# Nine more seven-product units in a two-block transformer forward pass on one NeuronCore

## The chip, the core and the metric

The kernel runs on one core of one Trainium2 chip. The metric is the device time of one execution in microseconds (us). Shorter is better.

## What is computed

Two blocks, on 256 tokens of width 2048, in float32. Cut to the matrix products that matter here:

```python
# first block
h = rms_norm(x, norm_mix_pre)
p, q, k, v, g_lr, r, gate_logits = split_combined(h @ w_in)      # 2048 x 11280
y_a = pool_mixer(p) @ w_branch_a                                 # 1024 x 2048
y_b = (rms_norm(gla(q, k, v, ...)) * silu(r)) @ w_branch_b        # 2048 x 2048
gates = sigmoid(gate_logits + b_branch_gates)                    # two gates of 2048 columns
mixed = (gates[0] * y_a + gates[1] * y_b) @ w_out                # 2048 x 2048
x = x + rms_norm(mixed)
h = rms_norm(x)
x = x + rms_norm((silu(h @ w_ffn_gate) * (h @ w_ffn_up)) @ w_ffn_down)   # 2048 x 5632
# second block, twice
z = rmsnorm(x) @ w_in_2[l]
y = concat(mla_attention, short_gated_conv, memory_attention) * silu(gate)
x = x + rmsnorm(y @ w_o_2[l])                                    # 2048 x 2048
```

## The kernel before

**Steps.** Each big product is a row of groups, each 512 output columns wide: `ga0` to `ga3` and `gb0` to `gb3` are the two gates, `ya`/`yb` the branches, `wo` the product with `w_out`, `fg`/`fu` feed-forward's gate and up, `d` its down product, `o00` to `o13` the output products of the two layers of the second block. `weight_groups` (line 98) writes them down in order. A step is one k-tile (128 rows) of one group. Both operands are split in a high and a low half of float32 (fp32r), so that a step is 3 matmuls (high by high, low by high, high by low; lines 1120 to 1122) for each of the two halves of the tokens: 6 matmuls of 128x512. Before, there are 1600 steps.

**Slabs.** Weights come in by DMA in pieces of 128x1024 (two k-tiles) into six `raw` buffers. For every piece, a slab, ScalarE (ACT) copies the high half into `wh` (line 1671) and VectorE (DVE) subtracts it to make the low half `wl` (line 2523). There are four slots for slabs, so that ACT can begin a slab only when TensorE (PE) has ended the one four places before. ACT and DVE each go through the slabs in order and between two slabs do what else is due: `background` and `results` are generators that yield a step number, and what follows a yield is put in the engine's queue ahead of the first slab that lies more than three slabs (`AHEAD`) beyond that step. So the order within each engine's queue is fixed when the program is built.

**Units.** In feed-forward, 16 times, the first four k-tiles of two neighbouring groups are not multiplied as 16 quarter products (8 steps) but as 7 (Winograd's form of Strassen's method), in 7 steps: `b11`, `b21`, `t1`, `t3`, `b22`, `t2`, `t4` (`FORMS`). A step of a unit is also 6 matmuls (lines 1041 to 1043), but has a slab of its own. So a unit has 7 slabs where 8 steps had 4. For the `t` slabs DVE first forms differences of raw weights in place (line 2517, four to a unit). The activations' sums and differences (`sform`) are made once for each set of four k-tiles by `forms` on DVE (five operations at lines 1798 to 1805, then the low half at line 1809) with `forms_high` on ACT between. In `seven` (line 1008) the first product `b11`, and every later one whose output lies in a bank `pb`, waits for semaphore `s_l`, the low half of these forms. Four products land in the banks `pb4` to `pb7`; `first_taken` (ACT, line 1206) and `gathered` (DVE, line 1811, four additions) add them up, and `joined` (line 1829) adds what the remaining k-tiles gave.

**The places of the change.** After each `yb` group DVE multiplies its result by the gate (line 2398), adds the two branches (line 2402), and, except after `yb3`, turns the sum with 16 small transposes (`turn`, lines 1688 to 1699) and makes its low half. After `yb3` it computes the tables of angles (`rope_tables`, line 1925) and the last low halves of `mixT`, the input of `wo` (line 1727). During `o00` and `o01` DVE and ACT also split the memory's activations (`memory_low`, `memory_high`). The results of `wo0` to `wo2` and `o00` to `o02` are squared by ACT and multiplied from the accumulator by DVE (`scaled_out`, line 1773).

Of the kernel before, what the change touches and what calls it, by code (L numbers as in the profile page):

```python
# [86 lines left out]
class Group:  # L87
# [3 lines left out]
    def __init__(self, name, act, cols, kts, per=2, gain=None, swap=False, ev=("d", 2)):  # L91
# [3 lines left out]
        self.pair = self.joins = self.forms = None  # L95


def weight_groups(a):
# [29 lines left out]
    def gate_up(part):
        c0, n = PARTS[part]
        w_g, w_u = a["w_ffn_gate"][0], a["w_ffn_up"][0]  # L130
        for c in range(c0, c0 + n):
# [4 lines left out]
            add(f"fu{c}", "x2T", w_u, 512 * c, kts=kts)

    def down(part):
        c0, n = PARTS[part]
        rows = a["w_ffn_down"][0][c0 * 512:(c0 + n) * 512, :]  # L140
        for c in range(4):
            if part < 3 and c % 2 == 0:
                seven(f"ds{part}{c}", f"fT{part % 2}", (f"d{part}{c}", f"d{part}{c + 1}"),
                      [rows[:, 512 * i:512 * i + 512] for i in (c, c + 1)], part + 1)
            add(f"d{part}{c}", f"fT{part % 2}", rows, 512 * c, kts=range(4 if part < 3 else 0, 4 * n), ev=("d", 2))
# [2453 lines left out]
```

## Time and profile before

| | |
|---|---|
| median of 3 runs | 2280.22 us (2280.21 to 2281.05) |
| the profiled execution, its own time | 2281.4 us |
| its span, first to last instruction | 2279.4 us |
| PE busy | 2267.1 us, 10645 instructions |
| DVE busy | 1648.4 us, 2158 instructions |
| ACT busy | 1227.9 us, 1599 instructions |
| granted TensorE clock, mean | 0.999 |

The profiled execution took 1.2 us more than the median, and 2.0 us of it lie outside the span. A matmul's recorded duration (389 ns) overlaps the next one's; the pace is the distance from one start to the next. The same holds for DVE, where one operation's record overlaps the next by some 0.08 us.

### The profile page before, as it was taken

How to read it: one execution, taken by the hardware profiler on the slowest of the kernel's cores; microseconds unless marked ns; L12 is line 12 of the kernel's file. 1: busy time of each engine (PE TensorE's matmuls, PEld its weight loads, DVE VectorE, ACT ScalarE, POOL GpSimd, SP SyncE). 2: the span in 40 equal slices, each digit the busy share in tenths (PEclk: the TensorE clock that was granted, in tenths of full speed). 3: DMA queues.
4: the chain of work that ended last, by engine and by line, in shares of the span. 5: the costliest groups of instructions: out<-in, count | busy, mean ns of one | idle time of the engine just before them, and what ended most of it. 6: DMA issues, size and time to landing. Idle time of an engine off the chain costs nothing.

```text
span 2279.4 us, 27834 instructions
## 1 busy us (share of the span) xinstructions
PE 2267.1 (99%) x10645; PEld 1897.2 (83%) x10645; DVE 1648.4 (72%) x2158; ACT 1227.9 (54%) x1599; POOL 30.5 (1%) x40
## 2 busy tenths in 40 slices
PE   9999999999999999999999999999999999999998
PEld 7888888888888888888888888888888888888887
DVE  6677777756666668898888988875668756676864
ACT  6555655444445755555555555565655446556443
POOL 0000000000000000000000000000000000000000
PEclk9999999999999999999999999999999999999999
DMA  8666665766668557756665776766565665656654
GB/s 295 179 194 197 194 192 166 228 202 202 194 202 275 176 163 251 241 192 226 219 200 174 244 228 213 251 206 197 160 180 166 223 209 148 203 163 182 173 198 136
DMA packets 261604, 458.34 MB, mean 201 GB/s; under 512 B 23808, under 2 KB 63744, under 8 KB 260832
## 3 DMA queue, kind: packets, MB, share of 16 engines
q1 hardware_dynamic: 260192, 453.94, 63.8%
q0 software_dynamic: 848, 2.10, 0.6%
q8 instruction: 84, 1.38, 0.2%
q10 hardware_dynamic: 432, 0.53, 0.1%
q14 instruction: 48, 0.39, 0.1%
HBM read 437.09 MB, written 4.19 MB: 194 GB/s over the span
## 4 chain that ended last, share of the span: by engine, by line
PE 92%; DVE 5%; DMA 1%; ACT 1%; issue 1%; SPq 0%; DVEq 0%; ACTq 0%
PE pm L1120 27%; PE pm L1122 27%; PE pm L1121 27%; PE pb L762 1%; DVE wl L2509 1%; DVE wl L2523 1%; PE pb L1041 1%; PE pb L944 1%; PE pb L1042 1%; PE pb L1043 1%; DVE raw L2517 1%; PE pm L1042 1%; PE pm L1041 1%; PE pm L1043 1%; PE pb L842 1%
## 5 line engine op out<-in xcount | busy, mean ns | idle before, releaser
L2523 DVE TENSOR_TENSOR wl<-raw,wh 128x1024 fp32r<-128x1024 f32 (+2 forms) x722 | 866.2, 1208 | 500.0 <-ACT wh L1671 496.8
L1671 ACT ACTIVATE wh<-raw 128x1024 fp32r<-128x1024 f32 (+2 forms) x722 | 749.4, 1044 | 734.8 <-PE pm L1122 665.0
L1120 PE MATMUL pm<-wh,hTh 128*128 128x512 f32 x702 | 275.1, 392 | 0.8 <-DVE wl L2523 0.8
L1121 PE MATMUL pm<-wl,hTh 128*128 128x512 f32 x702 | 273.3, 389 | 0.0
L1122 PE MATMUL pm<-wh,hTl 128*128 128x512 f32 x702 | 273.3, 389 | 0.0
L1120 PE MATMUL pm<-wh,xT3h 128*128 128x512 f32 (+1 forms) x640 | 249.0, 389 | 0.0
L1122 PE MATMUL pm<-wh,xT3l 128*128 128x512 f32 (+1 forms) x640 | 244.6, 382 | 0.0
L1121 PE MATMUL pm<-wl,xT3h 128*128 128x512 f32 (+1 forms) x640 | 244.4, 382 | 0.0
L1120 PE MATMUL pm<-wh,x2Th 128*128 128x512 f32 x544 | 211.6, 389 | 0.0
L1121 PE MATMUL pm<-wl,x2Th 128*128 128x512 f32 x544 | 211.6, 389 | 0.0
L1122 PE MATMUL pm<-wh,x2Tl 128*128 128x512 f32 x544 | 211.6, 389 | 0.0
L1666 ACT ACTIVATE wh<-raw 128x1024 fp32r<-128x1024 f32 x112 | 118.7, 1061 | 116.7 <-PE pm L1122 87.3
L1120 PEld LDWEIGHTS pm<-wh,hTh 128*128 128x128 f32 x702 | 131.8, 188 | 28.8 <-DVE wl L2523 2.2
L1122 PEld LDWEIGHTS pm<-wh,hTl 128*128 128x128 f32 x702 | 131.8, 188 | 27.7
L1121 PEld LDWEIGHTS pm<-wl,hTh 128*128 128x128 f32 x702 | 131.9, 188 | 26.5
L2509 DVE TENSOR_TENSOR wl<-raw,wh 128x1024 fp32r<-128x1024 f32 x112 | 135.4, 1220 | 18.6 <-ACT wh L1666 17.5
L1122 PEld LDWEIGHTS pm<-wh,xT3l 128*128 128x128 f32 x640 | 120.1, 188 | 23.1
L1121 PEld LDWEIGHTS pm<-wl,xT3h 128*128 128x128 f32 x640 | 120.4, 188 | 20.4
L1120 PEld LDWEIGHTS pm<-wh,xT3h 128*128 128x128 f32 x640 | 120.4, 188 | 20.5
L1120 PEld LDWEIGHTS pm<-wh,x2Th 128*128 128x128 f32 x544 | 102.1, 188 | 21.3
L1122 PEld LDWEIGHTS pm<-wh,x2Tl 128*128 128x128 f32 x544 | 102.1, 188 | 21.2
L1121 PEld LDWEIGHTS pm<-wl,x2Th 128*128 128x128 f32 x544 | 102.1, 188 | 21.1
(512 smaller groups left out, 3760.8 us busy)
## 6 DMA issues: line engine op xcount, KB each, us to landing
raw<-in_w_in SPq DMA_DIRECT2D x286, 512.0 KB, 4.0
raw<-in_w_ffn_gate SPq DMA_DIRECT2D x88, 512.0 KB, 4.9
raw<-in_w_ffn_up SPq DMA_DIRECT2D x88, 512.0 KB, 5.7
raw<-in_w_ffn_down SPq DMA_DIRECT2D x88, 512.0 KB, 5.1
raw<-in_w_o SPq DMA_DIRECT2D x64, 512.0 KB, 4.3
raw<-in_w_in SPq DMA_DIRECT2D x68, 256.0 KB, 3.3
raw<-in_w_branch_b SPq DMA_DIRECT2D x32, 512.0 KB, 4.2
raw<-in_w_out SPq DMA_DIRECT2D x32, 512.0 KB, 4.5
```

The source lines that it names most:

```text
L762: ins = e.transpose(pb[b][:, o:o + 128], src[half], ident[:, :])
L842: ins = e.matmul(pb[4 + i][:, j * 128:j * 128 + 128], E[:, 4 * i + j, 0, ft, :], E[:, 4 * i + j, 1, ft, :], start=(ft == 0), stop=(ft == 1))
L1041: e.matmul(out, lhs[0][k], h[:, cols], start=(k == 0), stop=False)
L1042: e.matmul(out, lhs[0][k], l[:, cols], start=False, stop=False)
L1043: ins = e.matmul(out, lhs[1][k], h[:, cols], start=False, stop=bool(b) and k == 1)
L1120: e.matmul(o, ah[:, kk, t], h[:, c], start=first and half >= joined, stop=False)
L1121: e.matmul(o, ah[:, kk, t], l[:, c], start=False, stop=False)
L1122: ins = e.matmul(o, al[:, kk, t], h[:, c], start=False, stop=last)
L1666: e.activation(h[:, :], r[:, :], ACT.Copy).then_inc(s["hi"], 1)
L1671: e.activation(h[:, 0:n], r[:, 0:n], ACT.Copy).then_inc(s["hi"], 1)
L2509: e.tensor_tensor(l[:, :], r[:, :], h[:, :].bitcast(F32), ALU.subtract).then_inc(s["lo"], 1)
L2523: e.tensor_tensor(l[:, 0:n], r[:, 0:n], h[:, 0:n].bitcast(F32), ALU.subtract).then_inc(s["lo"], 1)
```

## The change

A function `pair` writes down a unit and the rest of its two groups, and nine pairs more use it:

- `gs1`, `gs2`, `gs3`: the gates `ga1`/`gb1` to `ga3`/`gb3`, over k-tiles 0 to 3.
- `ws0`, `ws2`: the four groups of `wo`.
- `fs0`: `fg0`/`fu0`.
- `os00`, `os02`, `os10`: `o00` to `o03` and `o10`/`o11`, over k-tiles 12 to 15.

In `ws0`, `fs0`, `os00` and `os10` (`middle`) the unit comes after the other 12 k-tiles of its first group; in the others it comes first, as in the 16 units before. There are now 1591 steps and 879 slabs (852 before). `forms` and `forms_high` are done for four more inputs (`hT`, `mixT`, and `yT` twice). The results of `gs` units are gathered in the buffers of the gates, those of `ws` and `os` in `WO` and `WO2`, the place of the output; so they are added to the accumulators by `joined`, squared by ACT from there (`sums_squares`, in the place of `out_squares`), and multiplied in place by `scaled`.

```diff
--- before.py
+++ after.py
@@ -54,7 +54,8 @@
 SUMS = {"b11": ("t1", 0, 1, 0), "b21": ("t3", 1, 3, 1), "t1": ("t2", 0, 3, 0), "b22": ("t4", 2, 2, 0)}
 SHAPED = (4, 6, 9)
 PRODUCT, SQUARED, CARRIED, SPLIT, GATHERED, LATER = 9, 11, 14, 27, 7, 14
-KO = (12, 13, 14, 15, 0, 1, 2, 3, 4, 5, 8, 9, 10, 11, 6, 7)
+KO = (12, 13, 14, 15, 0, 1, 2, 3, 4, 5, 6, 7, 8, 9, 10, 11)
+SHAPES = {"gs": 0, "ws": 1, "fs": 2, "ds": 3, "os": 6}
...
+    def pair(unit, act, names, blocks, ks=k16, middle=False):
+
+        ks = list(ks)
+        if middle:
+            add(names[0], act, blocks[0], 0, kts=ks[4:])
+        out.append(Group(unit, act, [(blocks[0], 512)], ks[:4], ev=None))
+        out[-1].pair, out[-1].joins, out[-1].middle = [[(w, 512)] for w in blocks], names, middle
+        if not middle:
+            add(names[0], act, blocks[0], 0, kts=ks[4:])
+        add(names[1], act, blocks[1], 0, kts=ks[4:])
...
     for c in range(4):
-        add(f"ga{c}", "hT", w_in, 7184 + 512 * c)
-        add(f"gb{c}", "hT", w_in, 9232 + 512 * c)
+        if c:
+            pair(f"gs{c}", "hT", (f"ga{c}", f"gb{c}"), [w_in[:, o + 512 * c:o + 512 * c + 512] for o in (7184, 9232)])
+        else:
+            add("ga0", "hT", w_in, 7184)
+            add("gb0", "hT", w_in, 9232)
         add(f"ya{c}", "paT", a["w_branch_a"][0], 512 * c, kts=range(8), ev=("d", 1))
         add(f"yb{c}", "oT", a["w_branch_b"][0], 512 * c, ev=("d", 1))
-    for c in range(4):
-        add(f"wo{c}", "mixT", a["w_out"][0], 512 * c, ev=("a" if c == 3 else "d", 2))
+    for c in (0, 2):
+        pair(f"ws{c}", "mixT", (f"wo{c}", f"wo{c + 1}"), [a["w_out"][0][:, 512 * i:512 * i + 512] for i in (c, c + 1)],
+             middle=not c)
...
         for c in range(c0, c0 + n):
-            if c:
-                seven(f"fs{c}", "x2T", (f"fg{c}", f"fu{c}"), [w[:, 512 * c:512 * c + 512] for w in (w_g, w_u)], 0)
-            kts = range(4 if c else 0, 16)
-            add(f"fg{c}", "x2T", w_g, 512 * c, kts=kts, ev=("d" if c else "a", 2))
-            add(f"fu{c}", "x2T", w_u, 512 * c, kts=kts)
+            pair(f"fs{c}", "x2T", (f"fg{c}", f"fu{c}"), [w[:, 512 * c:512 * c + 512] for w in (w_g, w_u)], middle=not c)
...
-        for c in range(4):
-            add(f"o{l}{c}", "yT", w_o, 512 * c, kts=KO, ev=("a" if (l, c) == (0, 3) else "d", 2))
+        for c in (0, 2):
+            if (l, c) < (1, 2):
+                pair(f"os{l}{c}", "yT", (f"o{l}{c}", f"o{l}{c + 1}"), [w_o[:, 512 * i:512 * i + 512] for i in (c, c + 1)],
+                     KO, middle=not c)
+            else:
+                add("o12", "yT", w_o, 1024, kts=KO)
+                add("o13", "yT", w_o, 1536, kts=KO)
...
             if b:
                 free(b)
-                bank[b] = ("q_c", u) if b == 4 else ("q_d", 4 * u)
-                w.wait_ge(s["s_l"], g.forms + 1)
-            elif form != "t4":
+                bank[b] = ("q_c", u) if b == 4 else ("q_d", p.gathers[g.name] + 4)
+                w.wait_ge(s["s_l"], p.shape(g.name) + 1)
+            elif form == "b22" or form == "b21" and not g.middle:
                 w.wait_ge(s[f"ev_{before.ev[0]}"], p.evac[before.name] - (form == "b22"))
+            whole = b or g.middle and form in ("b21", "t4")
             for k in range(2):
                 cols = slice(512 * k, 512 * k + 512)
-                e.matmul(out, lhs[0][k], h[:, cols], start=(k == 0), stop=False)
+                e.matmul(out, lhs[0][k], h[:, cols], start=(k == 0 and (bool(b) or not whole)), stop=False)
                 e.matmul(out, lhs[0][k], l[:, cols], start=False, stop=False)
-                ins = e.matmul(out, lhs[1][k], h[:, cols], start=False, stop=bool(b) and k == 1)
+                ins = e.matmul(out, lhs[1][k], h[:, cols], start=False, stop=bool(whole) and k == 1)
             ins.then_inc(s["mm"], 1)
...
         yield at0
-        if n:
-            w.wait_ge(s["f_l"], 2 * PARTS[n - 1][0] + 2)
+        if n == 0:
+            w.wait_ge(s["oT_l"], 16)
+            w.wait_ge(s["d_zo"], 1024)
+        if n == 1:
+            w.wait_ge(s["rp_a"], 2)
...
+            sem, value = ready(p, act, k0 + 3, l)
+            w.wait_ge(s[sem], value)
+        if n >= 6:
+            w.wait_ge(s["mm"], p.end[f"gb{l}_"])
+        h, l = (x[:, k0:k0 + 4, :] for x in m.acts[act])
...
+        yield p.end[name] + (1 if name[0] == "o" else 2 if name[0] != "f" else GATHERED + 4 if name == "fs9" else GATHERED)
...
+        w.wait_ge(s["mm"], p.done[name])
+        w.wait_ge(s["q_d"], p.gathers[unit] + 4)
+        e.tensor_tensor(C if into is None else into, C, banks(name)[:, half, :], ALU.add
+                        ).then_inc(s["q_d" if unit[0] == "g" else "ev_d"], 1)
+
+    def scaled(dst, name, bc, loads):
+
+        c = int(name[-1])
+        w.wait_ge(s["sq"], SQ[name])
+        w.wait_ge(s["d_bc"], loads)
+        for half in range(2):
+            e.tensor_tensor(dst[:, half, part(c)], dst[:, half, part(c)], bc[:, part(c)], ALU.mult).then_inc(s["fs_d"], 1)
...
+        O, loads = p.first[f"o{l}0"], 48 + 16 * l
+        yield from forms(6 + l, O + 5)
         if l == 0:
-            yield p.end["o03"]
+            yield from memory_low(1, 0)
+            yield from memory_low(1, 1)
+        w.wait_ge(s["pv"], 12 * l + 12)
+        yield from gathered(f"os{l}0")
+        for half in range(2):
+            joined(f"os{l}0", 0, half)
+        if l == 0:
+            yield from memory_low(1, 2)
+        yield O + 26
+        scaled(m.WO2, f"o{l}0", m.BC3, loads)
+        if l == 0:
+            yield from memory_low(1, 3)
+        yield p.end[f"o{l}1"]
+        for half in range(2):
+            joined(f"os{l}0", 1, half)
+        yield p.end[f"o{l}1"] + 5
+        scaled(m.WO2, f"o{l}1", m.BC3, loads)
...
+                    if c:
+                        joined(f"gs{c}", br, half)
+                        w.wait_ge(s["q_d"], p.gathers[f"gs{c}"] + 5 + 2 * br + half)
+                    e.scalar_tensor_tensor(G[:, half, :], G[:, half, :] if c else acc[:, half, :],
+                                           m.rs["x"][:, half:half + 1], m.BI[br][:, :], ALU.mult, ALU.add
+                                           ).then_inc(s["ev_d"], 1)
...
+                yield from forms(0, p.end["v3"] + 58)
...
                 yield from turn(G0, p.end[f"yb{c}"] + 2, "mx_r", "mix_d", c + 1)
+                yield from gathered(f"gs{c + 1}")
                 for i in range(2):
                     yield p.end[f"yb{c}"] + 12 + i
                     low_turned(i, m.mixT, 4 * c + 2 * i, "mix_h", 2 * c + i + 1, "mix_l")
...
+        E = p.end["yb3"]
+        yield from forms(1, E + 8)
+        yield from gathered("ws0")
+        for half in range(2):
+            joined("ws0", 0, half)
+        yield E + 28
+        scaled(m.WO, "wo0", m.BC, 16)
+        yield p.end["wo1"]
+        for half in range(2):
+            joined("ws0", 1, half)
+        for i in range(4):
+            if i == 0:
+                yield E + 36
+                scaled(m.WO, "wo1", m.BC, 16)
+            if i == 2:
+                yield from gathered("ws2")
+            yield E + 37 + 2 * i
+            w.wait_ge(s["mem_h"], i + 1)
+            e.tensor_tensor(m.memT[1][:, 4 * i:4 * i + 4, :], m.memR[i][:, :, :],
+                            m.memT[0][:, 4 * i:4 * i + 4, :].bitcast(F32), ALU.subtract).then_inc(s["mem_l"], 1)
...
+        for half in range(2):
+            joined("ws2", 1, half)
+        yield p.end["wo3"] + 3
         variance("wo", DM, SQ["wo3"])
```

**Place 1.** DVE's queue where the branches of columns 0 to 511 end (`yb0`). `stg` are the gates' buffers, `turned` is what the transposes write. Before:

```order
L2398 TENSOR_TENSOR stg_127<-pm,stg_127 128x1024
L2523 TENSOR_TENSOR wl_67<-raw_57,wh_63 128x1024
L2402 TENSOR_TENSOR stg_126<-stg_126,stg_127 128x1024
L1699 STREAM_TRANSPOSE turned<-stg_126 32x2x4x32 x2
L2523 TENSOR_TENSOR wl_64<-raw_58,wh_60 128x1024
L1699 STREAM_TRANSPOSE turned<-stg_126 32x2x4x32 x4
L2523 TENSOR_TENSOR wl_65<-raw_59,wh_61 128x1024
L1699 STREAM_TRANSPOSE turned<-stg_126 32x2x4x32 x4
L2523 TENSOR_TENSOR wl_66<-raw_54,wh_62 128x1024
```

Here a slab (line 2523) lasts two steps of PE, and every slab has at most four transposes beside it. Now, with unit `gs1` in this place (line 2629 is the low half of a unit's slab, line 2637 a sum of raw weights):

```order
L2508 TENSOR_TENSOR stg_127<-pm,stg_127 128x1024
L2629 TENSOR_TENSOR wl_67<-raw_55,wh_63 128x1024
L2512 TENSOR_TENSOR stg_126<-stg_126,stg_127 128x1024
L2629 TENSOR_TENSOR wl_64<-raw_57,wh_60 128x1024
L2637 TENSOR_TENSOR raw_56<-raw_56,raw_54 128x1024
L1761 STREAM_TRANSPOSE turned<-stg_126 32x2x4x32 x2
L2629 TENSOR_TENSOR wl_65<-raw_54,wh_61 128x1024
L1761 STREAM_TRANSPOSE turned<-stg_126 32x2x4x32 x2
L2629 TENSOR_TENSOR wl_66<-raw_56,wh_62 128x1024
L1761 STREAM_TRANSPOSE turned<-stg_126 32x2x4x32 x2
L2643 TENSOR_TENSOR wl_67<-raw_58,wh_63 128x1024
L1761 STREAM_TRANSPOSE turned<-stg_126 32x2x4x32 x2
```

The gate's product (now line 2508) and the addition (2512) now stand among the unit's slabs. Every two transposes share one slab of the unit; the other transposes and the four additions of `gathered` follow among the next four slabs. The same order stands at `gs2` and `gs3`.

**Place 2.** DVE's queue after `yb3`, where `wo0` runs. Before:

```order
L1727 TENSOR_TENSOR mixTl<-pb,mixTh 128x512
L2523 TENSOR_TENSOR wl_66<-raw_54,wh_62 128x1024
L1727 TENSOR_TENSOR mixTl<-pb,mixTh 128x512
L2523 TENSOR_TENSOR wl_67<-raw_55,wh_63 128x1024
L2523 TENSOR_TENSOR wl_64<-raw_56,wh_60 128x1024
```

Now, from the slab of `ws0`'s first product `b11` on:

```order
L2637 TENSOR_TENSOR raw_54<-raw_55,raw_54 128x1024
L1789 TENSOR_TENSOR mixTl<-pb,mixTh 128x512
L1872 TENSOR_TENSOR shape_188<-mixTh,mixTl 128x1024
L1874 TENSOR_TENSOR shape_189<-shape_188 128x256
L1875 TENSOR_TENSOR shape_189<-shape_188 128x256
L1877 TENSOR_TENSOR shape_189<-shape_189,shape_188 128x256
L1879 TENSOR_TENSOR shape_189<-shape_188,shape_189 128x256
L2629 TENSOR_TENSOR wl_64<-raw_56,wh_60 128x1024
L2637 TENSOR_TENSOR raw_55<-raw_57,raw_55 128x1024
L2629 TENSOR_TENSOR wl_65<-raw_54,wh_61 128x1024
L2637 TENSOR_TENSOR raw_54<-raw_57,raw_54 128x1024
L1882 TENSOR_TENSOR shape_187<-shape_189,shape_186 128x1024
```

The row ahead of these is the slab of `b11` itself. Three sums, two slabs and the five operations of `forms` now stand between it and line 1882, the low half of the forms. On PE `b11` waits for that (`s_l`), as the queue of PE at this place shows:

```order
L1157 MATMUL pm<-wh_62,mixTl 128x512
L1155 MATMUL pm<-wh_62,mixTh 128x512
L1156 MATMUL pm<-wl_66,mixTh 128x512
L1157 MATMUL pm<-wh_62,mixTl 128x512
L1075 MATMUL pb<-wh_63,mixTh 128x512 [waits s_l,q_c,lo]
L1076 MATMUL pb<-wl_67,mixTh 128x512
```

**Place 3.** DVE's queue in `os00` (layer 0), between the forms' low half and the product `t2`:

```order
L1882 TENSOR_TENSOR shape_199<-shape_201,shape_198 128x1024
L1983 SCALAR_TENSOR_TENSOR memB0l<-memS_165,gain,memB0h 128x256 x4
L2629 TENSOR_TENSOR wl_66<-raw_58,wh_62 128x1024
L2637 TENSOR_TENSOR raw_58<-raw_55,raw_58 128x1024
L2629 TENSOR_TENSOR wl_67<-raw_59,wh_63 128x1024
L1983 SCALAR_TENSOR_TENSOR memB0l<-memS_166,gain,memB0h 128x256 x4
L2629 TENSOR_TENSOR wl_64<-raw_55,wh_60 128x1024
L2637 TENSOR_TENSOR raw_54<-raw_54,raw_58 128x1024
L2629 TENSOR_TENSOR wl_65<-raw_58,wh_61 128x1024
```

In this unit two `memory_low` (line 1983, four operations each) stand between its slabs as well. The place of the rows of line 1983 follows from when the memory's data are needed and hasn't changed against the steps.

## Rows read from the trace of the kernel before

**Rows 1.** The page: span, and busy time of each engine.
```profile
span 2279.4 us, 27834 instructions
...
PE 2267.1 (99%) x10645; PEld 1897.2 (83%) x10645; DVE 1648.4 (72%) x2158; ACT 1227.9 (54%) x1599; POOL 30.5 (1%) x40
```

**Rows 2.** The page: the chain that ended last, shares by engine.
```profile
PE 92%; DVE 5%; DMA 1%; ACT 1%; issue 1%; SPq 0%; DVEq 0%; ACTq 0%
```

**Rows 3.** PE's waits: waiter, releaser, total us, times, longest.
```profile
PE pb L1041 <- DVE wl L2509: 1.7, 4, 0.6
```

**Rows 4.** Windows of 100 us: PE, PEld, DVE, ACT, POOL busy, clock, DMA, GB/s.
```profile
500.00:600.00 100.00, 100.00 (x442) 82.79 (x442) 67.53 (x79) 42.41 (x41) 0.00 (x0) 1.00 0.66 195
...
900.00:1000.00 100.00, 100.00 (x443) 82.77 (x442) 84.33 (x87) 52.55 (x56) 0.00 (x0) 1.00 0.74 244
```

**Rows 5.** DVE in time order: unit fs1, and one row of unit fs4: start, length.
```profile
839.41 1.23 DVE L2509 TENSOR_TENSOR wl<-raw,wh 128x1024 fp32r<-128x1024 f32 x1 [0.30 <-ACT wh L1666]
...
841.69 1.41 DVE L2460 SCALAR_TENSOR_TENSOR fst<-pm,st,fst 128x512 f32<-128x512 f32 x2
843.01 2.35 DVE L2509 TENSOR_TENSOR wl<-raw,wh 128x1024 fp32r<-128x1024 f32 x2
...
846.41 2.50 DVE L2509 TENSOR_TENSOR wl<-raw,wh 128x1024 fp32r<-128x1024 f32 x2
...
1017.69 2.49 DVE L2509 TENSOR_TENSOR wl<-raw,wh 128x1024 fp32r<-128x1024 f32 x2
```

**Rows 6.** PE in time order: b11 of unit fs1, then t2 of unit fs4.
```profile
840.84 0.39 PE L1041 MATMUL pb<-wh,x2Th 128*128 128x512 f32 x1
...
1018.96 0.50 PE L1041 MATMUL pb<-wh,sform 128*128 128x512 f32 x1 [0.39 <-DVE wl L2509]
```

**Rows 7.** DVE in time order: four of the sixteen transposes after a yb group.
```profile
440.78 1.78 DVE L1699 STREAM_TRANSPOSE turned<-stg 32x256 f32<-32x256 f32 x4
```

**Rows 8.** Groups by line: one of the four additions of `gathered` (mean ns).
```profile
L1822 DVE TENSOR_TENSOR C<-C,pb 128x512 f32<-128x512 f32 x13 | 8.8, 680 | 0.0
```

**Rows 9.** DVE in time order: after yb3.
```profile
662.81 1.22 DVE L2402 TENSOR_TENSOR g<-g,g 128x1024 f32<-128x1024 f32 x1
667.59 0.17 DVE L1931 CAST st<-posi 128x2 f32<-128x2 int32 x1 [3.57 <-DMA invf<-in_cst]
...
675.28 1.22 DVE L2523 TENSOR_TENSOR wl<-raw,wh 128x1024 fp32r<-128x1024 f32 x1
676.41 0.68 DVE L1727 TENSOR_TENSOR mixTl<-pb,mixTh 128x512 fp32r<-128x512 f32 x1
```

**Rows 10.** PE in time order: yb3's last matmul, and the turns during wo0.
```profile
660.08 0.39 PE L1122 MATMUL pm<-wh,oT3l 128*128 128x512 f32 x1
667.12 0.60 PE L762 MATMUL pb<-ident,g 128*128 128x128 f32 x4
```

**Rows 11.** DVE in time order: `forms`, first and next operation after its five.
```profile
802.53 1.22 DVE L1798 TENSOR_TENSOR srows<-x2Th,x2Tl 128x1024 f32<-128x1024 f32 x1
...
805.26 1.22 DVE L2523 TENSOR_TENSOR wl<-raw,wh 128x1024 fp32r<-128x1024 f32 x1
```

**Rows 12.** DVE in time order: where o00 starts, and one `memory_low`.
```profile
1797.24 1.41 DVE L2179 SCALAR_TENSOR_TENSOR gt<-pm,st,gt 128x512 f32<-128x512 f32 x2
...
1806.58 2.36 DVE L2523 TENSOR_TENSOR wl<-raw,wh 128x1024 fp32r<-128x1024 f32 x2 [0.26 <-ACT wh L1671]
...
1813.12 1.67 DVE L1902 SCALAR_TENSOR_TENSOR memB0l<-memS,gain,memB0h 128x256 fp32r<-128x256 f32 x4
```

**Rows 13.** ACT in time order: the first `memory_high` during o00.
```profile
1809.28 1.71 ACT L1335 ACTIVATE memB0h<-memS,gain 128x256 fp32r<-128x256 f32 x4 [1.79 <-DMA memS<-in_memT]
```

**Rows 14.** Windows at the end, after PE's last matmul: columns as in Rows 4.
```profile
2272.00:2276.00 4.00, 0.30 (x2) 0.00 (x0) 2.84 (x6) 0.69 (x2) 0.55 (x1) 1.00 0.12 45
...
2277.00:2278.00 1.00, 0.00 (x0) 0.00 (x0) 0.00 (x0) 0.00 (x0) 0.00 (x0) 0.50 1.02 371
```

**Rows 15.** PE in time order: its first nine matmuls, 128x512.
```profile
1.32 4.21 PE L1048 MATMUL pb<-warm 128*128 128x512 f32 x9 [1.32 <-POOL warm L698]
```

More of the change, by code:

```diff
@@ L140, in down @@
         rows = a["w_ffn_down"][0][c0 * 512:(c0 + n) * 512, :]
-        for c in range(4):
[L142 to L145, printed above, removed]
+        if part == 3:
+            for c in range(4):
+                add(f"d3{c}", "fT1", rows, 512 * c, kts=range(4 * n))
+            return
+        for c in (0, 2):
+            pair(f"ds{part}{c}", f"fT{part % 2}", (f"d{part}{c}", f"d{part}{c + 1}"),
+                 [rows[:, 512 * i:512 * i + 512] for i in (c, c + 1)], range(4 * n))
     gate_up(0)
@@ L998, in background @@
         yield from mix_turns()
-        yield from row_sums(522, m.msum, "mrd", 5, "mss", "mem")
+        yield from row_sums(p.end["yb3"] + 58, m.msum, "mrd", 5, "mss", "mem")
         yield from mk_turns(0)
@@ L1121, in tensor_program @@
                     e.matmul(o, ah[:, kk, t], l[:, c], start=False, stop=False)
-                    ins = e.matmul(o, al[:, kk, t], h[:, c], start=False, stop=last)
+                    ins = e.matmul(o, al[:, kk, t], h[:, c], start=False, stop=last and g.name not in opened)
             if g.name != LAST:
@@ L1226, in out_squares @@
             squares(acc[:, half, :], m.ssq[key][:, half * 4 + c:half * 4 + c + 1])
-    def out_last(name, dst):
-        acc = m.pm[p.acc[name]]
-        for half in range(2):
-            e.activation(dst[:, half, part(3)], acc[:, half, :], ACT.Copy).then_inc(s["ev_a"], 1)
     def attention(l, r, which):
@@ L1454, in layer @@
                          ).then_inc(s["c_h"], 1)
-        for c in range(4):
-            if l == 0 and c < 2:
-                yield from memory_high(1, 2 * c)
-                yield from memory_high(1, 2 * c + 1)
-            yield p.end[f"o{l}{c}"] if (l, c) < (1, 2) else p.steps
-            if (l, c) < (1, 3):
-                out_squares(f"o{l}{c}", f"lay{l}", c)
-        if l == 0:
-            w.wait_ge(s["pv"], 12)
-            out_last("o03", m.WO2)
-        else:
+        O, key = p.first[f"o{l}0"], f"lay{l}"
+        yield from forms_high(6 + l, O + 8)
+        if l == 0:
+            yield from memory_high(1, 0)
+            yield from memory_high(1, 1)
+        yield from first_taken(f"os{l}0")
+        if l == 0:
+            yield from memory_high(1, 2)
+        yield O + 23
+        sums_squares(f"o{l}0", key, m.WO2)
+        if l == 0:
+            yield from memory_high(1, 3)
+            yield from first_taken("os02")
+        yield p.end[f"o{l}1"] + 3
+        sums_squares(f"o{l}1", key, m.WO2)
+        if l == 0:
+            for c in (2, 3):
+                yield p.end[f"o0{c}"] + 3 - (c == 3)
+                sums_squares(f"o0{c}", key, m.WO2)
+        else:
+            yield p.steps
+            out_squares("o12", key, 2)
             acc = m.pm[p.acc[LAST]]
@@ L1583, in background @@
                                  ).then_inc(s["rp_a"], 1)
-        for c in range(2):
-            yield p.end[f"wo{c}"]
-            out_squares(f"wo{c}", "wo", c)
+        E = p.end["yb3"]
+        yield from forms_high(1, E + 11)
+        yield from first_taken("ws0")
+        yield E + 24
+        sums_squares("wo0", "wo", m.WO)
+        yield from first_taken("ws2")
+        yield p.end["wo1"] + 3
+        sums_squares("wo1", "wo", m.WO)
         for c in range(4):
-            yield 500 + 2 * c
+            yield E + 36 + 2 * c
             w.wait_ge(s["mm"], p.end["gb3"])
```

269 lines of the change are left out of this document (144 added, 125 removed).

## The prediction

> **What bounds the kernel now.** Read first the busy times [rows 1] and the chain that ended last [rows 2]: TensorE (PE) is busy 99% of the span and makes 92% of the chain. Then the windows [rows 4]: in a window of 100 us PE starts 442 or 443 matmuls, one every 0.226 us, and this is the same where VectorE (DVE) is busy for 68% of the time and where it is busy for 84%. So a step of six matmuls takes 1.36 us, a slab of two steps 2.71 us, and a matmul less is 0.226 us less, **as long as DVE keeps up**. The waits of PE [rows 3] say how near that is: four times a unit's product waited for the low half of a slab on DVE, 1.7 us in all.
>
> Unit `fs1` shows the margin [rows 5, 6]. PE starts `b11` at 840.84; call that 0. DVE starts the low half of `t1` at -1.43 (it waited for ACT, which waits for a slot), then the third sum; at +0.85 it is free, puts two operations of 512 columns in (1.32 us), starts the low half of `t3` at 843.01, and `t2` at 846.41, which is +5.57. An operation of 128x1024 costs DVE 1.14 us from start to start (843.01 to 846.41 is three of them). In `fs4` the slab of `t2` begins at 1017.69 on DVE and its matmuls at 1018.96 on PE, which had been idle: from DVE's start to PE's start it takes **1.27 us**. So `t2` of `fs1` can start at +6.84, and it is due at 5 steps, +6.78. A unit bears 1.3 us of other work on DVE between `t1`'s sum and `t2`; each us more is a us of idle PE. The reason: in a unit's 9.5 us DVE has 7 low halves and 4 sums, 12.5 us; it lives on its lead of three slabs.
>
> **What is taken away.** Nine steps, 54 matmuls: 54 x 0.226 = **-12.2 us**. The order of PE's queue has exactly 54 fewer, so the change does what it says. The 27 slabs and 36 sums more, nine gatherings, four sets of forms and the longer way of `joined` and `scaled` lie on DVE and ACT, and cost nothing where a lead hides them. Where they stand between slabs decides.
>
> **Gate units, `gs1` to `gs3`** (place 1). Between the third sum (DVE free at +0.85) and the fifth slab after the unit, the queue now holds: the gate's product, the addition, low halves of `t3`, `b22`, `t2`, `t4`, the fourth sum, and four ordinary low halves: 11 x 1.14 = 12.5 us [rows 5, 9]; 16 transposes of 0.445 [rows 7] = 7.1; seven changes from a slab to a transpose, 0.12 each (1.26 instead of 1.14) = 0.8; four additions of 0.68 [rows 8], paced 0.62 = 2.5. The fifth slab begins at 0.85 + 22.9 = +23.8, and PE can use it at +25.0. It is due at 7 x 1.36 + 4 x 2.71 = +20.3. PE loses 4.7 us, three times: **+14.2**. Before, the same work stood beside slabs of 2.71 us, and no wait shows.
>
> **`ws0`** (place 2). In this order `b11` waits for the forms' low half. Up to the low half of `mixT` the queue is the old one: 675.28, and 676.41 plus one sum of 1.14 [rows 9]. Tables and `mixT` cannot come earlier, as DVE waits there until 667.59 for a DMA. From 677.55: 0.6 for `mixT`, 2.73 for the five operations [rows 11], four operations of 1.14, so line 1882 starts at 685.5, and `b11` can start 1.27 later, at 686.7. Due it is 12 steps after yb3 ended (660.08 + 0.23), plus 0.94 for two turns on PE (four transposes each, 0.60 long, of which 0.13 lies beside the matmul before [rows 10]; 2 x 0.47): 677.5. **+9.2 us**, after which DVE has enough lead for the rest of the unit.
>
> A PE idle that long may also lose its clock. From 2272 on it makes 0.30 us of its last matmuls and then idles; the granted clock was 1.00 (the level of 2.4 GHz) until 2276 and 0.50 (1.2 GHz) from 2277 [rows 14], so it fell when PE had idled for 4 to 5 us. What a cold start costs is shown at the beginning only: nine matmuls in 4.21 us [rows 15], about 2 us more than at 0.226 each. I add **+2.0** here; the bounds are 0 and 4. "TensorE: Matmul & The Clock Gate" in the Trainium skill (Part 1) gives this as a rule: after an idle window the array is clocked at half its rate until it has been busy again. The trace's end agrees with the fall; no row shows it in mid-kernel.
>
> **`os00`** (place 3). `o00` starts at 1797.1 [rows 12], so `b11` is due 12 steps and two turns later, at 1814.3. DVE starts the sixth slab at 1806.58, then forms (1807.7 to 1810.5), `b11`'s slab and sum. ACT copies the forms' high half (1.0) and then makes the memory's high half, 1.7 [rows 13], before it comes to `b21`: 1810.5 + 1.0 + 1.6 + 1.1 = 1814.2. Low half of `b21`, second sum, forms' low half start at 1814.2, 1815.4, 1816.5; `b11` starts at 1817.8, 3.5 late. Then come on DVE, from 1816.5: the forms' low half 1.1, a `memory_low` 1.6 [rows 12], `t1`, the third sum and `t3` 3.4, a `memory_low` 1.6, `b22` and the fourth sum 2.3. So `t2` starts at 1826.5 and is used at 1827.8, against 1817.8 + 6.8 = 1824.6: 3.2 more. **+6.7.** **`os10`** has no memory in it: forms' low half at 1815.0 on the same clock, 1816.3 against 1814.3, **+2.0**.
>
> **The other units**, by the margin of 1.3 us. `ws2`: `scaled` and two `joined`, 2.4 us, partly in a gap: +1.0. `os02`: the same and one `memory_low`, 4.0: +2.9. `fs0`: forms are ready in time (the first slab of the unit is due at 16.3 us after `fg0` starts, line 1798 comes 5 us after it, as before): 0. `fs1`: only `fu0` now lies between it and `fs0`, so `fs0`'s gathering (2.5) and two `joined` (1.2) stand before `b21`'s slab; with a gap of 1.2 and 0.6 for the third `joined`: +2.1. Together **+6.0**.
>
> Everything else (tail, layers' attention, the 15 later units) keeps its order; 0.
>
> **The sum:** -12.2 + 14.2 + 9.2 + 2.0 + 6.7 + 2.0 + 6.0 = +27.9. On the profiled execution's own 2281.4 that is 2309.3; it stood 1.2 above the median, so **2308**. The terms' bounds: clock 0 to 4, the six smaller units 8 to 20 instead of 14.7, `gs` 12 to 16. That makes 2298 to 2318 for this case.
>
> **Rivals.**
> - *DVE's lag stays hidden, as in the 16 units before.* Then only the 54 matmuls count: 2280.2 - 12.2 = 2268. For it: DVE is busy only 68% of the gates' stretch. Against it: the mean says nothing of the 20 us in which the queue holds 23 us of work. It would need the lead to be 5 us longer than four slots allow.
> - *Half of the idling.* If DVE's pace between small operations is better than I take it, or the DMA before the tables (3.57 us) lands sooner, 40 us of idling become about 22: 2290.
> - *Each stall cools the array.* If the shorter stalls at the three gate units and `os00` too drop the clock, 4 x 2 us more: 2316. The clock-gate page of the Trainium skill would allow it for `os00`'s 3.5 us of idling at most, and then the sum is 2310.
>
> **How the numbers follow.** Forecast as above 0.67; half the idling 0.14; more cooling 0.06; hidden 0.09; between hidden and half, near no change, 0.04. The forecast with its bounds and the cooling case hold 0.73; the range of 8 in 10 reaches down to take in the half case, with a few us for its own error: 2286 to 2318. A difference of 0.2% (4.6 us) is about what a measurement of this kernel can tell from none. Faster: 0.09; within: 0.04; slower: 0.87.
>
> **What would show it.** PE's waits: from line 1075 (unit products) on line 2629, some 25 us, and on the row of `ws0` one wait of about 9 us released by line 1882, with the granted clock below 1.00 in that slice. In windows of gate units fewer than 442 matmuls per 100 us. DVE's `t2` slab after two pairs of transposes. PE's instructions 54 fewer. It is wrong if PE is 100% busy from 400 to 660 us: then DVE did more in the time than its queue before shows.

## The result, and the profile after

The changed kernel takes **2316.5 us** (median of 5 runs, 2313.7 to 2317.2) against 2280.6 (5 runs): ratio 1.0154, 95% interval 1.0142 to 1.0166, so 35.9 us slower. 2308 was forecast, with 2286 to 2318 as the range.

The page of the changed kernel, and its chain:

```profile
span 2314.7 us, 28023 instructions
...
PE 2270.1 (98%) x10591; PEld 1889.1 (82%) x10591; DVE 1778.6 (77%) x2317; ACT 1259.9 (54%) x1635; POOL 29.8 (1%) x40
...
PE 82%; DVE 12%; DMA 2%; issue 2%; ACT 2%; SPq 0%; DVEq 0%; ACTq 0%
```

PE has 54 instructions fewer than in [rows 1] and yet is "busy" 3 us longer: a matmul's record runs 0.16 us past its pace, which counts once more for every stop, and some matmuls ran at the lower clock. What was lost is plainer in the chain, where DVE went from 5% [rows 2] to 12%, and in the waits (waiter, releaser, total us, times, longest):

```profile
PE pb L1075 <- DVE wl L2629: 11.5, 11, 1.8
PE pb L1075 <- DVE shape L1882: 10.7, 3, 5.4
PE pm L1155 <- DVE wl L2643: 7.2, 13, 0.9
PE pm L1155 <- DVE mixTl L1789: 3.4, 1, 3.4
PE pm L1075 <- DVE wl L2629: 2.0, 5, 0.5
```

In [rows 3] the first of these was 1.7 us, in four waits. The prediction named some 25 us on line 2629; it is 13.5, and line 2643, the ordinary slabs behind the units, has another 7.2. Windows of 100 us (columns as in [rows 4]):

```profile
500.00:600.00 100.00, 95.12 (x413) 76.64 (x412) 78.07 (x85) 45.88 (x47) 0.00 (x0) 1.00 0.52 166
900.00:1000.00 100.00, 100.00 (x443) 82.81 (x442) 86.17 (x87) 55.23 (x60) 0.00 (x0) 1.00 0.66 220
```

In the gates' stretch PE starts 413 matmuls instead of 442, at DVE 78% busy; in feed-forward 443, at DVE 86%. The mean of an engine does not tell whether it is late.

The stages, each from its first matmul to the next stage's, by PE's rows in time order. "Lost" is what remains once the matmuls removed are taken off at 0.226 us each:

| stage | before | removed | after | lost | forecast |
|---|---|---|---|---|---|
| gates and branches after `yb0` | 228.5 | 4.1 | 238.8 | 14.4 | 14.2 |
| `wo` | 88.5 | 2.7 | 99.6 | 13.9 | 12.2 |
| feed-forward | 701.6 | 1.4 | 703.0 | 2.7 | 2.1 |
| `o00` to `o03` | 88.0 | 2.7 | 97.9 | 12.6 | 9.6 |
| `o10` to `o13` | 87.8 | 1.4 | 90.2 | 3.8 | 2.0 |

All other stages are equal within 0.1 us. Lost 47.4, removed 12.2: +35.2, against +27.9 forecast. (The spans of the two profiles differ by 35.3.)

**Gates.** DVE in time order at unit `gs1`, whose `b11` starts at 431.84 (call it 0), then PE's rows that waited:

```profile
438.36 0.88 DVE L1761 STREAM_TRANSPOSE turned<-stg 32x256 f32<-32x256 f32 x2
439.25 1.23 DVE L2629 TENSOR_TENSOR wl<-raw,wh 128x1024 fp32r<-128x1024 f32 x1
440.51 0.89 DVE L1761 STREAM_TRANSPOSE turned<-stg 32x256 f32<-32x256 f32 x2
...
455.63 1.22 DVE L2643 TENSOR_TENSOR wl<-raw,wh 128x1024 fp32r<-128x1024 f32 x1
```

```profile
440.53 0.50 PE L1075 MATMUL pb<-wh,shape 128*128 128x512 f32 x1 [1.51 <-DVE wl L2629]
442.69 0.50 PE L1075 MATMUL pm<-wh,hTh 128*128 128x512 f32 x1 [0.51 <-DVE wl L2629]
444.84 0.50 PE L1155 MATMUL pm<-wh,hTh 128*128 128x512 f32 x1 [0.50 <-DVE wl L2643]
...
456.91 0.50 PE L1155 MATMUL pm<-wh,hTh 128*128 128x512 f32 x1 [0.87 <-DVE wl L2643]
```

The fifth slab after the unit begins at +23.8 on DVE and at +25.1 on PE, the places that the sum of the queue gave, and `t2` (440.53) starts 1.28 us after its low half did. The wait is spread over four slabs: the first three have two transposes before them, the last four transposes and the additions of `gathered`.

**`ws0`.** First DVE, then PE:

```profile
678.15 0.17 DVE L2012 CAST st<-posi 128x2 f32<-128x2 int32 x1 [3.78 <-DMA invf<-in_cst]
...
685.24 0.68 DVE L1789 TENSOR_TENSOR mixTl<-pb,mixTh 128x512 fp32r<-128x512 f32 x1
...
695.98 1.22 DVE L1882 TENSOR_TENSOR shape<-shape,shape 128x1024 fp32r<-128x1024 f32 x1
```

```profile
686.08 0.47 PE L1155 MATMUL pm<-wh,mixTh 128*128 128x512 f32 x1 [3.43 <-DVE mixTl L1789]
697.34 0.76 PE L1075 MATMUL pb<-wh,mixTh 128*128 128x512 f32 x1 [5.43 <-DVE shape L1882]
697.90 0.63 PE L1076 MATMUL pb<-wl,mixTh 128*128 128x512 f32 x1
```

Line 1882 starts 25.3 us after `wo0` began (25.2 in the sum). The 9.2 us come in two stops, 3.6 and 5.6 start to start: `wo0` now takes k-tile 12 at its 9th step, where before it was the 13th, and meets `mixT` unfinished: its low half, behind the tables, starts at 685.24. The prediction had not seen the first stop. The second is shorter by as much, since DVE's queue fixes when line 1882 starts.

**Output.** `b11` of `os00` and of `os10`:

```profile
1840.73 0.47 PE L1075 MATMUL pb<-wh,yTh 128*128 128x512 f32 x1 [3.38 <-DVE shape L1882]
...
2236.26 0.47 PE L1075 MATMUL pb<-wh,yTh 128*128 128x512 f32 x1 [1.89 <-DVE shape L1882]
```

3.5 and 2.05 us late from start to start (0.16 of each lies in the record of the matmul before), as forecast (3.5 and 2.0).

**The clock.** Windows of 4 us at `ws0`, `os00`, `os02` and `os10`. Of the last three numbers the first is the granted clock, the mean over the window:

```profile
696.00:700.00 4.00, 2.66 (x6) 2.15 (x7) 2.33 (x3) 0.00 (x0) 0.00 (x0) 0.50 0.00 0
...
1840.00:1844.00 4.00, 3.27 (x10) 2.57 (x11) 4.00 (x7) 1.67 (x3) 0.00 (x0) 0.71 0.20 52
1880.00:1884.00 4.00, 4.00 (x13) 3.12 (x13) 3.95 (x5) 3.07 (x3) 0.00 (x0) 0.67 0.34 92
...
2238.00:2242.00 4.00, 4.00 (x13) 3.15 (x12) 4.00 (x5) 2.60 (x3) 0.00 (x0) 0.62 0.01 2
```

Four falls from 1.00 (2.4 GHz) to 0.50 (1.2 GHz). The prediction had only the first in its sum; that one slowed ten matmuls, by 2.1 us. In the window of `os02` PE was busy throughout and started 13 matmuls where 4 us hold 17 or 18.

### The profile page after: what moved, and what is told of

Read it like the earlier page. It is cut to its first block, busy times and chain, and to the rows that moved or that the text cites. A ratio compares the mean times of both kernels' runs of the same rounds, so it can differ in the third digit from the quotient of the medians.

```text
span 2314.7 us, 28023 instructions
## 1 busy us (share of the span) xinstructions
PE 2270.1 (98%) x10591; PEld 1889.1 (82%) x10591; DVE 1778.6 (77%) x2317; ACT 1259.9 (54%) x1635; POOL 29.8 (1%) x40
## 4 chain that ended last, share of the span: by engine, by line
PE 82%; DVE 12%; DMA 2%; issue 2%; ACT 2%; SPq 0%; DVEq 0%; ACTq 0%
PE pm L1155 23%; PE pm L1157 23%; PE pm L1156 23%; DVE wl L2629 2%; DVE wl L2643 2%; DVE raw L2637 2%; PE pb L1075 1%; PE pb L791 1%; PE pb L1077 1%; PE pb L1076 1%; PE pb L973 1%; PE pm L1077 1%; PE pm L1075 1%; PE pm L1076 1%; DVE turned L1761 1%
## 5 line engine op out<-in xcount | busy, mean ns | idle before, releaser
L2643 DVE TENSOR_TENSOR wl<-raw,wh 128x1024 fp32r<-128x1024 f32 (+3 forms) x686 | 820.4, 1205 | 411.3 <-ACT wh L1733 407.6
L1733 ACT ACTIVATE wh<-raw 128x1024 fp32r<-128x1024 f32 (+3 forms) x686 | 710.7, 1043 | 657.9 <-PE pm L1157 559.4
L1728 ACT ACTIVATE wh<-raw 128x1024 fp32r<-128x1024 f32 x175 | 184.8, 1059 | 183.8 <-PE pm L1157 121.2
L1155 PE MATMUL pm<-wh,hTh 128*128 128x512 f32 x654 | 257.3, 393 | 5.2 <-DVE wl L2643 5.2
L1156 PE MATMUL pm<-wl,hTh 128*128 128x512 f32 x654 | 254.7, 389 | 0.0
L1157 PE MATMUL pm<-wh,hTl 128*128 128x512 f32 x654 | 254.6, 389 | 0.0
L2629 DVE TENSOR_TENSOR wl<-raw,wh 128x1024 fp32r<-128x1024 f32 x175 | 212.2, 1222 | 30.7 <-ACT wh L1728 29.4
L1155 PEld LDWEIGHTS pm<-wh,hTh 128*128 128x128 f32 x654 | 122.8, 188 | 34.0 <-DVE wl L2643 9.6
L1157 PEld LDWEIGHTS pm<-wh,hTl 128*128 128x128 f32 x654 | 122.8, 188 | 25.9
L2637 DVE TENSOR_TENSOR raw<-raw,raw 128x1024 f32<-128x1024 f32 x100 | 122.0, 1220 | 0.0
```

The costliest lines, as they stand in the source:

```text
L1155: e.matmul(o, ah[:, kk, t], h[:, c], start=first and half >= joined, stop=False)
L1156: e.matmul(o, ah[:, kk, t], l[:, c], start=False, stop=False)
L1157: ins = e.matmul(o, al[:, kk, t], h[:, c], start=False, stop=last and g.name not in opened)
L1728: e.activation(h[:, :], r[:, :], ACT.Copy).then_inc(s["hi"], 1)
L1733: e.activation(h[:, 0:n], r[:, 0:n], ACT.Copy).then_inc(s["hi"], 1)
L2629: e.tensor_tensor(l[:, :], r[:, :], h[:, :].bitcast(F32), ALU.subtract).then_inc(s["lo"], 1)
```

## Experiments

Where a result is called "less", it is against the changed kernel's 2316.5. The kernel before, measured again beside each set, took 2279.7 us beside e1 to e4, 2280.1 beside e5 to e7 and 2280.8 beside e8 and e9, against 2280.6 beside the changed kernel. So up to 0.9 us of such a difference can lie between the sets: against the kernel before beside them, e1 to e4 gained 15.6, 4.4, 9.2 and 5.3. The lengths of stages are from the profiles.

**e1, the turn behind the units.** The same instructions in another order: at a gate unit the queue holds no transposes, and the addition and the four additions of `gathered` come later.

```diff
@@ vector_program
+                if c and br == 0:
+                    yield from turn(m.ring[2 * ((c - 1) % 2)], p.end[name] + 2, "mx_r", "mix_d", c)
...
-            yield p.end[f"yb{c}"] + 1
+            yield p.end[f"yb{c}"] + (1 if c == 3 else 8)
...
-                yield from turn(G0, p.end[f"yb{c}"] + 2, "mx_r", "mix_d", c + 1)
                 yield from gathered(f"gs{c + 1}")
```

> The changed kernel with one thing moved at the gate units: the addition of the two branches stands behind the unit, and the 16 transposes of a turn wait until the next gate group is done (12 steps later); the same instructions, no fewer. Theory (DVE's queue is 4.8 us too long where the gate units stand): the three stalls of 4.8 us shrink to some 0.3 each, 13 to 14 us in all, so about 2303 us. Rival (a unit cannot be fed at this place whatever stands beside it: seven slabs in 9.5 us are too many for ACT, the slots or the DMA): no gain, 2316 us, and the waits on line 2629's place remain at the gate units.

Measured 2299.9 us, 16.5 less. The windows:

```profile
420.00:460.00 40.00, 40.00 (x178) 33.08 (x177) 33.01 (x33) 19.26 (x19) 0.00 (x0) 1.00 0.60 204
500.00:600.00 100.00, 100.00 (x443) 82.55 (x442) 84.03 (x90) 48.84 (x50) 0.00 (x0) 1.00 0.57 196
```

PE is full again with DVE busier than in the changed kernel (84% against 78%). The gates' stage takes 224.7 us; with every unit free it would be 228.5 - 4.1 = 224.4. The rival is out: seven slabs in 9.5 us can be fed there. In the profiles, 15.3 us apart in span, the gates give 14.1; 0.4 and 0.7 came in `wo` and at `o00` to `o03`, where the clock fell at other places (below): it did not fall at `os02`.

**e2, `b11` without the forms.**

```diff
-                w.wait_ge(s["s_l"], p.shape(g.name) + 1)
+                if form != "b11":
+                    w.wait_ge(s["s_l"], p.shape(g.name) + 1)
```

> The changed kernel, but a unit's first product b11, which does not read the forms, no longer waits for their low half; t1, the first that reads them, does. Theory (DVE's queue sets the times, the wait only shows them): at ws0 b11 and b21 (2.7 us) fill part of the idling, the second stop is 2.8 us instead of 5.6, and the fall of the clock (2 us) may go; at os00 the stop moves from b11 to t1, because t1's own low half is queued behind the memory's, and nothing but the clock's 1.6 us can be had; at os10 some 1.7 us of 3.7. Together -4 to -8 us: 2309 to 2312. Rival (the wait itself is the cost): the 5.6, 3.5 and 2.05 us of idling go with their clock, -15 us: 2301.

Measured 2311.2 us, 5.3 less. By stage: `wo` -3.8, `o00` to `o03` +0.2, `o10` to `o13` -1.7. The time lies in the range expected, and the rival is out. At `os00` the stop only changed its name. DVE's and PE's rows there (lines are one higher in this kernel), and a window behind:

```profile
1835.74 1.22 DVE L1883 TENSOR_TENSOR shape<-shape,shape 128x1024 fp32r<-128x1024 f32 x1
1836.87 1.67 DVE L1984 SCALAR_TENSOR_TENSOR memB0l<-memS,gain,memB0h 128x256 fp32r<-128x256 f32 x4
1838.46 1.22 DVE L2630 TENSOR_TENSOR wl<-raw,wh 128x1024 fp32r<-128x1024 f32 x1
```

```profile
1839.73 0.49 PE L1076 MATMUL pb<-wh,shape 128*128 128x512 f32 x1 [3.25 <-DVE wl L2630]
```

```profile
1844.00:1848.00 4.00, 4.00 (x11) 2.82 (x10) 3.95 (x4) 2.11 (x3) 0.00 (x0) 0.50 0.00 0
```

`t1`'s own low half stands behind `memory_low`, and PE starts it 1.27 us after. The unit's stops sum to 4.7 us instead of 5.0 (start to start beyond the pace); the clock was down here until 1848, in the changed kernel until 1845, and that took back more. At `os10` one stop of 2.05 us became three of 0.4, 0.8 and 0.6, and no fall came behind them: the 1.7 us gained are about what that fall had cost. Removing a wait that is last by little gives little when the queue behind it sets the time.

**e3, the gate units undone.** The forms of `hT` are still made.

```diff
-        if c:
-            pair(f"gs{c}", ...)
-        else:
-            add("ga0", "hT", w_in, 7184)
-            add("gb0", "hT", w_in, 9232)
+        add(f"ga{c}", "hT", w_in, 7184 + 512 * c)
+        add(f"gb{c}", "hT", w_in, 9232 + 512 * c)
```

> The changed kernel with the three gate units undone (their groups are multiplied in 16 + 16 steps as before; the forms of hT are still made, unused). The gate stage then is as before the change: 3 x 4.8 us of idling go and 3 x 1.36 us of matmuls come back, -10.4 us: 2306 us. If the gates' stalls had also delayed something later (the load lead, the tables after yb3), more than that would go, and the windows from yb3 on would differ from the changed kernel's.

Measured 2306.4 us, 10.1 less. The gates' stage is 228.5 us as before the change, and no later stage gains (`wo` 100.1, output 98.1 and 90.1), so the gates' stalls did nothing to what follows.

**e4, the memory's splittings behind the units.**

```diff
-MEM_FROM, ... ((1, 5, 12, 16), (8, 12, 20, 26))
+MEM_FROM, ... ((1, 5, 12, 16), (20, 24, 41, 46))
```

> The changed kernel with the four splittings of the memory's activations (memory_high on ACT, memory_low on DVE) and two of their loads moved behind the units: the first two from steps 8 and 12 of the output product to 20 and 24, the others from 20 and 26 to 41 and 46. Theory (they stand in the queues between the forms and the unit's slabs): b11 of os00 waits 2.0 us as in os10 instead of 3.5, the two small waits behind it (1.2 us) and the one row of drift go, -3 to -5 us: 2311.5 to 2313.5. Rival (os00 is late because its forms come late, the memory costs nothing): 2316.

Measured 2310.3 us, 6.2 less. `b11` of `os00` waits 2.04 us, as `os10` does, the two waits behind it are gone, and the stage takes 92.5 us instead of 97.9. Of these 5.4 us, DVE's order gives 2.9 (1.5 at `b11` and the two waits, 1.4), which is the theory. The rest is that the clock fell neither there, though PE stopped for 2 us, nor at `os02`, while at `os10` the same stop was followed by a fall:

```profile
1836.00:1840.00 4.00, 2.12 (x10) 1.49 (x9) 4.00 (x5) 2.16 (x3) 0.00 (x0) 1.00 0.01 5
1840.00:1844.00 4.00, 4.00 (x18) 3.28 (x18) 4.00 (x4) 2.46 (x3) 0.00 (x0) 1.00 0.00 0
2230.00:2234.00 4.00, 2.53 (x7) 2.04 (x8) 4.00 (x5) 1.15 (x2) 0.00 (x0) 0.76 0.00 0
```

Without a fall at `os02` PE stops once more in that unit, 0.6 us with the matmul behind it, which the changed kernel does not; e1 has the same row. There the slow matmuls had covered this stop:

```profile
1877.48 0.50 PE L1075 MATMUL pb<-wh,shape 128*128 128x512 f32 x1 [0.35 <-DVE wl L2626]
```

**e10, the changed kernel once more**, for the clock (one profile).

> The changed kernel itself, profiled once more, for the clock alone. In its first profile the clock fell behind four of the six stops of 2 us and more (5.6, 3.5, 2.05 and 1.95 us, not behind 3.6), and in e4 a stop of 2.04 us at os00 passed without. If the length of a stop decides, the same four fall again and the stops between are the same to 0.1 us. If it also hangs on when the stop comes, the set differs from one execution to the next while DVE's and PE's own stops stay; each fall then is 1.4 to 2.5 us of the spread between runs (2313.7 to 2317.2 us).

It took 2315.1 us. DVE's and PE's own stops came back to 0.1 us at the gates, `fs1`, `os00`, `os02` and `os10`; the falls did not. Behind the 2.04 us stop at `os10` the clock stayed:

```profile
2234.00:2238.00 4.00, 2.11 (x10) 1.46 (x9) 4.00 (x5) 1.13 (x2) 0.00 (x0) 1.00 0.00 0
2238.00:2242.00 4.00, 4.00 (x19) 3.31 (x18) 4.00 (x5) 2.50 (x3) 0.00 (x0) 1.00 0.02 6
```

and the stage took 88.6 us instead of 90.2. **Here one fall costs 1.6 us.** At `ws0` the clock fell at the first stop as well, and that cost nothing: PE's slow matmuls filled what had been idling, the second stop was 3.3 instead of 5.6 us, and `wo` took 99.3 us instead of 99.6.

**e5, more work out of the units' stretch.** e1, e2 and e4 together (the memory's splittings at steps 20, 40, 45 and 52), and besides, shortened:

```diff
-        yield E + 28
+                yield E + 39
         scaled(m.WO, "wo0", m.BC, 16)
...
-            yield E + 37 + 2 * i
+            yield E + (41, 44, 47, 49)[i]
...
-yield from squares_added(..., [E + x for x in (45, 47, 47, 48, 48)])
+yield from squares_added(..., [E + x for x in (51, 52, 53, 54, 55)])
...
-        yield p.end[name] + (... else GATHERED)
+        yield p.end[name] + (... else 2 if name == "fs0" else GATHERED)
```

> The three edits that moved work out of the units' stretch or dropped b11's wait, together (the turn after the gate group; b11 without the forms; the memory's splittings later), and three more of the kind: the results of wo0, wo1, o00 and o01 are scaled after unit ws2 or os02 instead of ahead of or inside it, the memory's activations of the first block are split three to four steps later, and fs0's results are gathered 2 steps after it instead of 7. Theory (each unit bears 1.3 us of other DVE work, each us beyond it is a us of idle PE): from the changed kernel's 2316.5, less 16.5, 5.3 and 6.2 as measured one by one, less 2.5 to 3 each for fs1 and os02 and 1 for ws2: 2282 to 2286 us; left are ws0's stops (about 3 and 2.8 us), os00's and os10's. Rival (what is moved out only makes the next stretch late): no more than the three edits give, 2288.5 or above.

Measured 2288.7 us, above the 2282 to 2286 expected. By the number this is the rival's, and in part it is. Against the kernel before beside them, the three edits alone would leave 10.6 us and e5 is at 8.6, so the rest gave about 2. Feed-forward fell to 700.5 us (`fs1`'s three waits are gone) and `o00` to `o03` to 89.5, but `wo` stayed at 99.4. The sum of the memory's squares was now late, and PE stopped 3.4 us for it. The clock fell at this stop and at `ws0`'s first. This wait stood in e6 and e7 too; in e7's list of waits:

```profile
PE pb L807 <- DVE msum L1834: 3.2, 1, 3.2
```

**e6, tables and forms early.**

```diff
-places of mixT's shapes: (200.5, 204.5, 212.5, 218)
+places of mixT's shapes: (RA + 24, RA + 28, RA + 8, RA + 12)
...
-        yield from forms(1, E + 8)
...
+            if c == 2:
+                yield from rope_tables()
+            if c == 3:
+                yield from forms(1, p.end["gb3"] + 1)
```

The tables' DMA is issued after `gb1`.

> The same, and what stands between yb3 and ws0 made early: the tables of angles with their DMA come in the third gate stretch (after gb2), and mixT's forms after gb3, into the space of hT, which is free by then. DVE then has between yb3 and the unit only the gate's product, the addition and two halves of mixT. Theory: both stops of ws0 (3 and 2.8 us) and the clock's 1 to 2 us go, 6 to 8 us: 2275 to 2279 us, at or just below the kernel before. Rival (the tables of 6.6 us in the gates' stretch make a stall there instead): 2282 or above, with a wait near gb2.

Measured 2284.4 us, 4.3 less instead of 6 to 8; this number too is the rival's. Both stops of `ws0` went (`wo` 93.1 us, 6.3 less), but two new stops of 1.2 and 1.1 us stand at the starts of `yb2` and `yb3`, behind the tables and the forms, so that the gates took 227.1 us instead of 224.8. The tables take DVE 4.8 us, not the 6.6 I had written (678.15 to 685.24 in the changed kernel, less two slabs).

**e7, the output's forms early.**

```diff
-        yield from forms(6 + l, O + 5)
+        shaping = forms(6 + l, O + 1)
+        yield next(shaping)
+        at = next(shaping)
...
+        yield at
+        yield from shaping
```

> The same, and the forms of the output products made 4 steps earlier, before the convolution's results. Theory: the stops at os00 and os10 (1 to 2 us each, with a fall of the clock) go; what is left of the change is 54 matmuls less and some 3 us of small waits: 2271 to 2275 us, faster than before by 5 to 9. Rival (the convolution's part is now late at k-tiles 8 to 11): as e6 or worse.

Measured 2281.2 us, not to be told from the kernel before (ratio 1.0005, 0.9995 to 1.0014), 3.2 less than e6, where 4 were expected. `o00` to `o03` takes 88.2 us and `o10` to `o13` 87.1 (85.3 and 86.4 would be without any wait). The level, 2271 to 2275, was missed by what e5 and e6 had missed; the step was nearly right. The profile is of the fastest of ten runs (2279.0): behind the memory's stop of 3.4 us the clock did not fall, as it had in e5 and e6.

**e8, the new waits mended** (shortened; the tables' and the forms' step numbers go with them).

```diff
-        yield from row_sums(p.end["yb3"] + 58, m.msum, "mrd", 5, "mss", "mem")
+        yield from row_sums(p.end["yb3"] + 61, m.msum, "mrd", 5, "mss", "mem")
...
+                if (c, br) == (2, 0):
+                    yield from rope_tables()
+                if (c, br) == (3, 0):
+                    yield from forms(1, p.end["ya3"] + 2)
```

> e7 with the three new waits that it made mended: PE's sum of the memory's squares, which waited 3.3 us for DVE (and cost the clock about 1 to 2 us behind it), comes 3 steps later, and the tables and mixT's forms stand after ya2 and ya3 instead of after gb2 and gb3, where the slabs at yb2 and yb3 were 1.2 and 1.1 us late. Theory: 3.4 + 1 to 2 + 2.3 us go: 2273.5 to 2275.5 us, 5 to 6.5 us under the kernel before. Rival (a program at the limit of DVE only moves its waits): 2279 or above, with new waits of the same sum at other places.

Measured **2273.5 us**, ratio 0.9969 (0.9958 to 0.9981): 7.3 us faster than the kernel before, with all nine units, at the lower edge of the times expected. Its waits:

```profile
PE pb L1077 <- DVE wl L2652: 2.1, 6, 0.5
PE pm L1157 <- DVE wl L2666: 2.0, 4, 0.7
```

Mean granted clock 0.999, DVE busy 78% of the span (77% in the changed kernel). By stage: gates 224.7, `wo` 87.1, feed-forward 699.3, output 88.2 and 87.1. Against the kernel before that is -3.8, -1.4, -2.3, +0.2 and -0.7, where the matmuls removed are 4.1, 2.7, 1.4, 2.7 and 1.4. So the gate units are hidden; those of `wo` and `os10` bring half of their matmuls, and `os00` and `os02` still wait away all that they save. About 1 us of feed-forward's 2.3 is not matmuls removed: the stops of 0.8 and 0.6 us at `fs2` in the kernel before are gone. No run has these moves without the nine units, so what the moves alone are worth stays open.

**e9, e8 with the gate units undone**, by the edit of e3.

> e8 without the three gate units (their groups multiplied in full, as before the change). If the units are hidden in e8, each is worth its step: 3 x 1.36 = 4.1 us slower than e8. If they still cost about what they save: the same as e8 within 1 us; if they cost more: faster.

Measured 2277.3 us, ratio 0.9985 (0.9976 to 0.9994): 3.8 slower than e8. The gates' stage is 3.8 longer too. Three hidden units are worth 3.8 us of the 4.1 that their matmuls take.

## Why the prediction came out so

- **What bounds the kernel, and the pace.** Right. 12.2 us of matmuls went, and every stage that the change does not touch kept its length.
- **Gate units, +14.2.** Right: 14.4, at the slabs and times that the queue gave. e1 shows the cause (the same instructions elsewhere cost 0.3 us), e3 that it stays in the stage. Only the sign named was off: part of it stands on line 2643, not 2629.
- **`ws0`, +9.2, and `b11` bound by line 1882.** Right in sum (9.2), with 3.6 of it at a wait that the prediction had not; "one wait of about 9 us" did not come. Taking the forms' wait away (e2) helped `wo` by 3.8 us.
- **`os00`, +6.7, and `os02`, +2.9.** The stage lost 12.6; less two falls of 1.6 that is 9.4, against 9.6. The agreement is a little flattered: in e1, without the fall at `os02`, the stage was only 0.7 us shorter, because another stop came in its place. So DVE's part is rather 10. That ACT's and DVE's memory splittings stand in the way is shown by e4 (2.9 us), and that the forms' wait alone costs little there by e2.
- **`os10`, +2.0.** 3.8 less one fall is 2.2.
- **`fs1`, +2.1, and `ws2`, +1.0.** Too low. `fs1` stopped PE for 1.7, 1.4 and 0.55 us, 3.6 in all. That the stage lost only 2.7 is luck: `fs2`'s 1.4 us of stops in the kernel before went, which the prediction had not. In `wo`, 13.9 - 9.2 - 2.0 leaves 2.7, of which 2.1 are stops at and behind `ws2`. I counted what stands between the third sum and `t2` only; waits of 0.5 and 0.6 us came at the ordinary slabs behind the unit too.
- **The step that failed: "Clock +2.0", one fall, at `ws0`.** There were three more, behind stops of 3.5, 1.95 and 2.05 us. At 1.6 each they are 4.8 of the 7.3 us by which the profiles' difference was missed; what they cost in the end is nearer 4, as the one at `os02` covers another stop. The rest is mostly `ws2` (2.7 for 1.0). "TensorE: Matmul & The Clock Gate" in the Trainium skill (Part 1) has the array fall after an idle window. I had read from that page that `os00` could fall at most, and the runs show falls behind stops of 2 us.
- **The rivals.** *Hidden*: out as written. e8 and e9 show that the gate units can be hidden, and that the order decides it; the output units of the first layer were hidden in no run. *Half the idling*: out, DVE's pace between small operations was as taken. *Each stall cools*: its 2316 is what was measured, but mostly not by its mechanism: of its four stops only `os00`'s cooled the array, the gates' (1.7 us at most) never, and two stops that it did not name did.
